# A two-block fp32 transformer on one core: two half groups at the end, a shorter first load, a conv tap moved to ACT and POOL, other planner durations

## What is computed

```python
def first_block(...):
    h = rms_norm(x, ln1)
    proj = h @ w_in                      # qkv_a, beta, decay, z, qkv_b, two gates
    y_a = gated_deltanet(qkv_a, ...) @ w_branch_a   # starts with the 4-tap conv below
    y_b = moba_attention(...) @ w_branch_b
    x = x + (sigmoid(gate_a) * y_a + sigmoid(gate_b) * y_b) @ w_out
    ...                                  # FFN with a 3-tap conv
def gated_deltanet(qkv, ...):
    qkv = silu(causal_dwconv(qkv, conv_w))          # 4 taps along the tokens, 3072 channels
    ...                                  # heads, chunks of 64 tokens
def second_block(...):
    z = rms_norm(x, attn_norm) @ w_in    # pool branch, RWKV7 with 16 heads
    x = x + concat(pool_out, rwkv_out) @ w_out
    x = x + square(relu(h2 @ w_ffn_up)) @ w_ffn_down
    gate = sigmoid(rms_norm(x, ple_norm) @ w_ple_gate)
    x = x + gate * (p @ w_ple_proj)
    return rms_norm(x, final_norm)
```

## Time and profile before

| | |
|---|---|
| median of 3 runs | 3005.75 us (3005.21 to 3009.81) |
| the profiled execution | 3008.47 us, its span 3006.7 us |
| mean granted clock of PE | 0.982 of full speed |
| busy: PE, DVE, ACT, POOL | 97%, 63%, 49%, 5% |
| read from HBM | 476.53 MB, 159 GB/s over the span |

### The profile page before, as it was taken

How to read it: one execution, slowest core, us unless ns; L and a number is a source line. 1 busy time by engine, 2 the same in 40 slices (tenths; PEclk the granted TensorE clock), 3 DMA queues, 4 the chain that set the end, 5 groups by cost and what they waited for, 6 DMA issues and landing times.

```text
span 3006.7 us, 55479 instructions
## 1 busy us (share of the span) xinstructions
PE 2919.0 (97%) x23504; PEld 2849.2 (95%) x23504; DVE 1908.6 (63%) x2146; ACT 1464.9 (49%) x1871; POOL 160.9 (5%) x136
## 2 busy tenths in 40 slices
PE   7998999999999999999999999998899999999998
PEld 7988989999999999999998999996899999999997
DVE  6467766555666667666777676664665555655665
ACT  5345555444554444444446555654544444444464
POOL 0010011000000000000001011111000000000000
PEclk9999999999999999999999999996999999999999
DMA  6644533665556665666565533330466666666654
GB/s 207 189 123 139 162 92 94 187 183 171 188 177 189 183 182 182 187 184 179 176 186 161 176 113 103 115 93 1 140 185 184 183 181 184 183 181 185 184 173 134
DMA packets 252104, 482.22 MB, mean 160 GB/s; under 512 B 16944, under 2 KB 22320, under 8 KB 251728
## 3 DMA queue, kind: packets, MB, share of 16 engines
q1 hardware_dynamic: 251856, 478.68, 53.2%
HBM read 476.53 MB, written 2.10 MB: 159 GB/s over the span
## 4 chain that ended last, share of the span: by engine, by line
PE 86%; DVE 7%; ACT 4%; DMA 2%; issue 1%; POOL 0%; DVEq 0%; SPq 0%; ACTq 0%; POOLq 0%
PE psm L411 78%; PE psb L470 7%; DVE slo L325 2%; DMA raw<-in_w_in 2%; ACT shi L315 1%; DVE ar L506 1%; DVE ar L498 1%; ACT ar L495 1%; PE psb L478 1%; DVE x L498 0%; ACT gf L495 0%; DMA raw<-in_w_out 0%; ACT L495 0%; DVE ar L509 0%; POOL ar L498 0%
## 5 line engine op out<-in xcount | busy, mean ns | idle before, releaser
L325 DVE TENSOR_TENSOR slo<-raw,shi 128x1024 fp32r<-128x1024 f32 (+1 forms) x901 | 1122.6, 1251 | 692.6 <-ACT shi L315 689.5
L315 ACT ACTIVATE shi<-raw 128x1024 fp32r<-128x1024 f32 (+1 forms) x901 | 946.6, 1054 | 1136.5 <-PE psm L411 897.2
L411 PE MATMUL psm<-gh,shi 128*128 128x256 f32 x3664 | 1050.7, 287 | 20.9 <-DVE slo L325 19.7
L411 PE MATMUL psm<-gl,shi 128*128 128x256 f32 x3664 | 1039.2, 284 | 0.0
L411 PE MATMUL psm<-gh,slo 128*128 128x256 f32 x3664 | 1039.1, 284 | 0.0
L411 PE MATMUL psm<-hh,shi 128*128 128x256 f32 x3408 | 974.5, 286 | 11.1 <-DVE slo L325 6.4
L411 PE MATMUL psm<-hh,slo 128*128 128x256 f32 x3408 | 966.4, 284 | 0.0
L411 PE MATMUL psm<-hl,shi 128*128 128x256 f32 x3408 | 966.4, 284 | 0.0
L411 PEld LDWEIGHTS psm<-gh,shi 128*128 128x128 f32 x3664 | 704.5, 192 | 28.7 <-DVE slo L325 22.6
L411 PEld LDWEIGHTS psm<-gl,shi 128*128 128x128 f32 x3664 | 704.6, 192 | 0.9 <-issue 0.3
L411 PEld LDWEIGHTS psm<-gh,slo 128*128 128x128 f32 x3664 | 704.1, 192 | 0.3
(11 more groups left out here) (190 smaller groups left out, 1304.9 us busy)
## 6 DMA issues: line engine op xcount, KB each, us to landing
raw<-in_w_in SPq DMA_DIRECT2D x240, 512.0 KB, 3.7
raw<-in_w_up SPq DMA_DIRECT2D x176, 512.0 KB, 4.0
raw<-in_w_ffn_up SPq DMA_DIRECT2D x128, 512.0 KB, 3.8
raw<-in_w_ffn_down SPq DMA_DIRECT2D x128, 512.0 KB, 4.2
raw<-in_w_down SPq DMA_DIRECT2D x88, 512.0 KB, 4.5
raw<-in_w_out SPq DMA_DIRECT2D x64, 512.0 KB, 4.2
raw<-in_w_ple_gate SPq DMA_DIRECT2D x32, 512.0 KB, 4.6
raw<-in_w_branch_b SPq DMA_DIRECT2D x16, 512.0 KB, 3.9
```

Of the source, the lines that this page charges most:

```text
L315: hi_tok[j] = A.do(lambda e: e.activation(shi[:, s, 0:m], raw[:, q, 0:m], ACT.Copy), landed, pe_tok.get(j - NS), chain=False, cost=0.22 + ...
L325: lo_tok[j] = V.do(lambda e: e.tensor_tensor(slo[:, s, 0:m], raw[:, q, 0:m], shi[:, s, 0:m].bitcast(F), ALU.subtract), landed, hi_tok[j], ...
L411: e.matmul(out, l, r, start=st, stop=sp, skip_group_check=True),
```

## The change

Four edits.

**Tail.** The last `pg` group of 512 columns becomes two of 256 columns. A tile then holds 4 blocks of rows by 256 columns: still 512 KB and still eight tiles, but rows of 1 KB instead of 2 KB in HBM. Each half has its own epilogue (`epi_half`). The sum of the earlier squares and of those of the first half is a background step (`sum_half`); the second half adds only its own. The last quarter of the output is scaled and stored in two pieces.

**Head.** The first load of `x` is split: blocks 0 and 1, weight tile 0, blocks 2 and 3, tile 1, then as before.

**Conv.** Tap 1 is no longer on DVE. Four more ACT scaled copies write it to `cth`, and one POOL tensor_tensor of 128 x 4 x 255 adds it to `dst`.

**Costs.** ACT's base goes from 0.22 to 0.25 us (0.33 with a scale from a tile), DVE's from 0.16 to 0.20, POOL's from 0.25 to 0.30, and scalar_tensor_tensor gets 0.05 more.

```diff
+            if g < 3:
+                gplan("pg", io["w_ple_gate_2"][0], 0, 512 * g, 512, 16)
+        for i in range(2):
+            gplan("pg", io["w_ple_gate_2"][0], 0, 1536 + 256 * i, 256, 16, kc=4)
...
-            return 0.25 + 2.0e-3 * columns(ap) if q is P else 0.16 + 1.04e-3 * columns(ap)
+            return 0.3 + 2.05e-3 * columns(ap) if q is P else 0.2 + 1.04e-3 * columns(ap)
...
         for f in range(4):
-            t_x.append(load(x[:, 4 * f:4 * f + 4, :], io["xt"][:, 4 * f:4 * f + 4, :]))
+            if f == 0:
+                t_x0 = load(x[:, 0:2, :], io["xt"][:, 0:2, :])
+                issue(0)
+                t_x.append(load(x[:, 2:4, :], io["xt"][:, 2:4, :]))
+                continue
             if f < NR:
                 issue(f)
+            t_x.append(load(x[:, 4 * f:4 * f + 4, :], io["xt"][:, 4 * f:4 * f + 4, :]))
...
                 for s in range(4):
-                    if s:
+                    o = dst if s == 0 else cth
+                    if s > 1:
...
                     for f in range(4):
-                        tq = act(dst[:, f, :], craw[:, f, :], ACT.Copy, tv, tt_["conv"],
-                                 scale=W("conv", 3 * 24 + 4 * g + f, 1))
+                        ta = act(o[:, f, s:256], craw[:, f, 0:256 - s], ACT.Copy, tv, tt_["conv"], g_tok.get(g - 1), tq,
+                                 scale=W("conv", (3 - s) * 24 + 4 * g + f, 1))
+                    if s:
+                        tq = tt(dst[:, :, s:256], dst[:, :, s:256], cth[:, :, s:256], ALU.add, ta, q=P)
                     yield
...
+        def sum_half():
+            while nf.n < 3 or 2 not in xw_tok:
+                yield
+            yield (x_tok[3], nf.tp[0])
+            sq = nf.sq[:, 0:512]
+            tq = act(sq.rearrange("p (a b) -> p a b", a=2), x[:, 12:14, :], ACT.Square, x_tok[3], nf.tp[0])
+            weigh((12, 13), 3, x_tok[3])
+            yield (tq,)
             b = bank()
...
+            mms([(b.ap[:, 0:256], C("ones"), s[:, 256 * k:256 * k + 256], k == 0 and s is nf.acc[0], False)
+                 for s, n in ((nf.acc[0], 4), (sq, 2)) for k in range(n)], nf.tp[0], tq, *b.free)
```

More of the change, by code:

```diff
@@ L213, in build @@
         s_raw = [sem(f"s_raw{i}") for i in range(NR)]
-        s_in = [sem(f"s_in{i}") for i in range(19)]
+        s_in = [sem(f"s_in{i}") for i in range(20)]
         s_out = sem("s_out")
@@ L483, in build, with acost @@
         table = [None]
-        def acost(ap, fn=ACT.Copy):
+        def acost(ap, fn=ACT.Copy, scale=1.0):
             own = {ACT.Sqrt: 1, ACT.Sin: 2, ACT.Ln: 3, ACT.Exp: 0, ACT.Tanh: 0}.get(fn, table[0])
@@ L488, in acost @@
             table[0] = own
-            return load + 0.22 + 0.82e-3 * columns(ap)
+            return load + (0.25 if isinstance(scale, float) else 0.33) + 0.82e-3 * columns(ap)
         def vcost(ap, q=None):
-            return 0.25 + 2.0e-3 * columns(ap) if q is P else 0.16 + 1.04e-3 * columns(ap)
+            return 0.3 + 2.05e-3 * columns(ap) if q is P else 0.2 + 1.04e-3 * columns(ap)
         def act(out, in_, fn, *tokens, scale=1.0, **kw):
-            return A.do(lambda e: e.activation(out, in_, fn, scale=scale, **kw), *tokens, cost=acost(out, fn))
+            return A.do(lambda e: e.activation(out, in_, fn, scale=scale, **kw), *tokens, cost=acost(out, fn, scale))
         def tt(out, a, b, op, *tokens, q=None):
@@ L505, in stt @@
         def stt(out, a, s, b, o1, o2, *tokens):
-            return V.do(lambda e: e.scalar_tensor_tensor(out, a, s, b, o1, o2), *tokens, cost=vcost(out))
+            return V.do(lambda e: e.scalar_tensor_tensor(out, a, s, b, o1, o2), *tokens, cost=0.05 + vcost(out))
         def rec(o, *tokens):
@@ L766, in build @@
         for j in range(NS):
-            nm.split((2 * j, 2 * j + 1), t_x[j // 2])
+            nm.split((2 * j, 2 * j + 1), t_x[j // 2] if j else t_x0)
             split_hi(j)
@@ L1059, in conv @@
                     for f in range(4):
-                        tq = act(dst[:, f, :], craw[:, f, :], ACT.Copy, tv, tt_["conv"],
-                                 scale=W("conv", 3 * 24 + 4 * g + f, 1))
+                        ta = act(o[:, f, s:256], craw[:, f, 0:256 - s], ACT.Copy, tv, tt_["conv"], g_tok.get(g - 1), tq,
+                                 scale=W("conv", (3 - s) * 24 + 4 * g + f, 1))
+                    if s:
+                        tq = tt(dst[:, :, s:256], dst[:, :, s:256], cth[:, :, s:256], ALU.add, ta, q=P)
                     yield
-                ta = act(cth, dst, ACT.Tanh, tq, g_tok.get(g - 1))
+                ta = act(cth, dst, ACT.Tanh, tq)
                 yield
+                V.wait(tq)
                 g_tok[g] = stt(dst, cth, 1.0, dst, ALU.add, ALU.mult, ta)
@@ L1860, in build, with weigh @@
         xw_tok = {}
-        def weigh(f):
-            for k in range(4 * f, 4 * f + 4):
-                xw_tok[f] = act(x[:, k, :], x[:, k, :], ACT.Copy, x_tok[f], scale=W("fn2", k, 1))
+        def weigh(ks, f, tok):
+            for k in ks:
+                xw_tok[f] = act(x[:, k, :], x[:, k, :], ACT.Copy, tok, scale=W("fn2", k, 1))
         def sum_up(f):
             yield from nf.squares(f, x_tok[f])
-            weigh(f)
+            weigh(range(4 * f, 4 * f + 4), f, x_tok[f])
             yield ()
@@ L1883, in epi_pg @@
             return epi
-        def epi_last(ps, tp):
-            bg_until(lambda: nf.n == 3 and 2 in xw_tok)
-            b = bank()
[L1889 to L1906, removed]
-                          for k in range(2)], tq)
[L1908 to L1911, removed]
@@ new lines, in build @@
+        last_sum = []
+        def sum_half():
[6 more added lines that the diff above has]
+            yield (tq,)
+            b = bank()
+            mms([(b.ap[:, 0:256], C("ones"), s[:, 256 * k:256 * k + 256], k == 0 and s is nf.acc[0], False)
+                 for s, n in ((nf.acc[0], 4), (sq, 2)) for k in range(n)], nf.tp[0], tq, *b.free)
+            last_sum.append(b)
+            yield ()
@@ new lines, in epi_half, with epi @@
+        def epi_half(i):
+            def epi(ps, tp):
+                bg_until(lambda: last_sum or not i)
+                th, xx = thb[:, 2 * i:2 * i + 2, :], x[:, 12 + 2 * i:14 + 2 * i, :]
+                tv = tt(th, ps[:, 0:512].rearrange("p (a b) -> p a b", a=2), bc(rb, 2), ALU.mult, tp)
+                ta = act(th, th, ACT.Tanh, tv, scale=0.5)
+                if i:
+                    act(pp1, C("eps", 0, 1), ACT.Sqrt)
+                stt(th, th, 1.0, ppb[:, 2 * i:2 * i + 2, :], ALU.add, ALU.mult, ta, pp_tok[-1])
+                x_tok[3 + i] = stt(xx, th, 0.5, xx, ALU.mult, ALU.add)
+                if not i:
+                    bgs[2].append(sum_half())
+                    return (tv,)
+                b, sq = last_sum[0], nf.sq[:, 512:1024]
+                tq = act(sq.rearrange("p (a b) -> p a b", a=2), xx, ACT.Square, x_tok[4])
+                tm = mms([(b.ap[:, 0:256], C("ones"), sq[:, 256 * k:256 * k + 256], False, k == 1)
+                          for k in range(2)], tq)
+                tr = act(rb, b.ap[:, 0:256], ACT.Sqrt, tm, scale=1.0 / D, bias=C("eps", 0, 1))
+                weigh((14, 15), 4, x_tok[4])
+                rec(rb, tr)
+                return (tv,)
+            return epi
@@ L1913, in build @@
         for g in range(4):
             group("pp", act_g(8), epi_pp, needs=(t_pp,))
-            group("pg", act_h, epi_pg(g) if g < 3 else epi_last)
+            if g < 3:
+                group("pg", act_h, epi_pg(g))
+        for i in range(2):
+            group("pg", act_h, epi_half(i))
+        parts = [(4 * f, 4 * f + 4, xw_tok[f]) for f in range(3)] + [(12, 14, xw_tok[3]), (14, 16, xw_tok[4])]
         tf = []
-        for f in range(4):
-            xx = x[:, 4 * f:4 * f + 4, :]
-            tf.append(tt(xx, xx, bc(rb, 4), ALU.mult, xw_tok[f]))
+        for a, e, t in parts:
+            tf.append(tt(x[:, a:e, :], x[:, a:e, :], bc(rb, e - a), ALU.mult, t))
@@ L1920, in build @@
         out_v = io["out"].rearrange("(c p) t -> p c t", p=128)
-        for c in range(4):
-            SP.dma(lambda e, c=c: e.dma_start(out_v[:, 4 * c:4 * c + 4, :], x[:, 4 * c:4 * c + 4, :]), s_out, tf[c])
+        for (a, e, _), t in zip(parts, tf):
+            SP.dma(lambda q, a=a, e=e: q.dma_start(out_v[:, a:e, :], x[:, a:e, :]), s_out, t)
             nout[0] += 1
```

1 line of the change is left out of this document (removed).

## The result

The changed kernel takes 3017.72 us (median of 5 runs, 3016.33 to 3021.73) beside 3005.75 us before (median of 5, 3002.57 to 3015.05); the ratio is 1.0031, interval 1.0018 to 1.0044. The two medians lie 12.0 us apart, more than the ratio says, so I go by ratio and interval. So it is 8 to 9 us slower. I had forecast 3008.4, no change, in a range from 2999 to 3016: the first median lies 1.7 us above its top, the second inside it, and the likeliest case (3005 to 3013) did not come true. Single runs of the kernel before spread from 2998 to 3018 us, so a stage's share has to be read from several traces.

The account below looks back on a forecast made before the run. PE, busy 97%, bounds the kernel: only its work, pauses and lowered clock count. Head 0, conv 0, reordered background 0, drain +2.4 and tail +0.2 give +2.6 on the median 3005.75: 3008.4 us, range 2999 to 3016.

Parts of the forecast that it names:

- the likeliest case: Whole kernel: the predicted sum of terms holds, 3005 to 3013 us; chance 0.50.
- Reordered background: 0: Background steps placed later by the new costs: small matmuls' sum unchanged, so 0 us, from −6 to +2.
- The conv: 0: Conv stretch, 204 to 345 us: moving tap 1 to ACT and POOL costs 0 us, from −3 to +12.
- the conv stretch gets shorter or longer by over 4 us: Sign that the prediction is wrong, for the stretch from 204 to 345 us.
- POOL's add locks DVE: Rival, conv: about four of six adds delay low splits by 2.1 us each; +8 to +12 us, 3015 to 3020; chance 0.15.
- The drain: 2023.7 to 2113 us: the output step stands 24 `psm` matmuls later and its chain keeps its length; +2.4 us, −3 to +6.
- The tail: Kernel end: six `psb` ahead of the last `psm` add 2.8 us, shorter work behind saves 2.5; +0.2, −0.8 to +1.5.
- The head: Kernel start: PE begins up to 1.0 us earlier but waits as much longer for the norm sum; 0, −1.0 to +0.3.

Follow-up runs that it names:

- The two removal runs: Costs and conv edits together on the kernel before, once with one ACT copy for tap 1's four (1.0015), once with tap 1's add on DVE, not POOL (1.0024).

## Why the prediction was right or wrong

**The step that failed: "Reordered background: 0".** I took the costs' reordering as a sum of small matmuls that stays the same, and priced only the waits (14.3 us missing in two stretches, of which some could be won). Means over the table's kernels give, for the new costs: from tile 54 to 132 333.2 us with the old conv for 336.8 with the old costs, −3.6; from 504 to 603 +3.7 (425.2 for 421.5). The second loss is not in a wait. As far as the traces tell it is the clock (13.7 us more at half), for which my step had no term: PE's pauses stay nearly as they were, but the matmuls came in lumps. My upper end of +2 was too low. The sum of the small matmuls is indeed the same, but not in each stretch: with the new costs the trace has 942 records of them from tile 504 to 603 where it had 972 or 976, and 382 in the drain for 354 (two records for each small matmul), while ten weight matmuls more stand ahead of tile 603. So the +3.7 came in spite of somewhat less work, and only the sum over the second block, below, can be compared.

**The second failure: that conv and costs add up.** "The conv: 0" holds with the old costs: 337.5 against 336.8 us. With the new costs the tap costs 7.3 us (340.5 against 333.2), and so takes back the costs' gain twice over. In whole runs the same interaction shows as 1.0025 for both edits beside 1.0002 and 0.9994 for each. By my own sign ("the conv stretch gets shorter or longer by over 4 us") I was wrong here too: tiles 54 to 132 took 4.1 and 6.6 us longer in the two traces of the changed kernel than in that of before. My working took one group's order and looked at the high split between the two sets of copies; there the split came first. In other groups a norm step stood in the same gap. The two removal runs gave back 5.0 us (fewer copies, and one locked low split less) and 3.2 us (no lock) in one trace each. They are not independent, since each shortens the same wait of PE, and in whole runs only the first may have given something back (1.0015, and 1.0024 for the second, beside 1.0025). So the tap behind the new order is shown as the cause in this stretch, and its division between copies and lock is not.

**The rival "POOL's add locks DVE"** had the right sign and size, 8 to 12 us, and its first condition came true (five low splits of six, where it wanted four). That it came near the measured time is luck: it was not the cause as stated, since each hit costs 1.3 us, not 2.1, with the old costs five such hits cost nothing, and part of the measured loss lies in the second block, where the conv is not. By the Trainium skill's rule (SBUF — State Buffer, Who interferes with whom) the second to be issued is fully blocked: the trace agrees, as the low split that started 0.98 us into POOL's add ended 1.08 us behind it, nearly its whole usual length. But what the block costs depends on whether PE waits behind it.

**The drain** was right in what moves and in part wrong in the rest. The chain goes through the output step in the changed kernel too, now right behind the last weight matmul:

```profile
2033.35 2.26 PE psb L473 x22
...
2035.99 1.28 ACT L498
```

In all six traces with the old costs this step starts 6.1 us ahead of the end of the last weight matmul, with 24 of them behind it; in the eight others it starts with that end. Predicted was +2.4 from the 24 weight matmuls; the means are 90.2 us for 86.7, +3.5, or +2.5 with the end of the stretch ahead of it (−1.0). That 2.5 is so near to 2.4 is partly luck, since the chain did not keep its length as I took it to: from the step to the next weight matmul it takes 90.2 us instead of 92.8. With the old costs that length goes from 89.6 to 95.4 us, and the half clock in it from 39 to 57 us. Behind the drain about 1.5 us came back: up to tile 880 it took 806.9 us and not 808.4. The clock does not explain this, it is at half for 5.1 us there for 5.0; PE is idle for 1.8 us instead of 3.1.

**The tail**: the term for six matmuls was 2.8 and measured 2.7 (67.9 for 65.2). Behind the last matmul I predicted 5.5 and the mean is 5.5, but the 8.0 us of before that I set against it was one execution with the clock at half. The mean of nine kernels with the old end is 6.9. So the gain was 1.5, not 2.5, and the tail is +1.2 instead of +0.2, in agreement with 1.0004. Taking a price at half clock from a single trace was the error.

**The head** was right in the mechanism: what PE gains at the start it waits longer. PE starts at 8.29 (predicted near 8.5) and waits 5.29 us for the norm sum instead of 4.59, and that wait ends 0.3 us later than before. Its price of 0 is not shown, since the head alone measured 3.6 us slower (interval 0.0 to 7.2):

```profile
8.29 0.58 PE L414 MATMUL psm<-gh,shi 128*128 128x256 f32 x1 [8.29 <-DVE slo L328]
...
39.97 1.62 PE L473 MATMUL psb<-ar,con 128*128 128x256 f32 x3 [5.29 <-DVE ar L501]
```

**The account.** First block +3.7 (340.5 for 336.8), RWKV stretch +3.7, its end −1.0 (from tile 603 to the drain 3.9 us for 4.9), drain +3.5, behind it −1.5, tail +1.2: +9.6 us. Left out are the head and the 372 tiles between the first two stretches, which took 1077.8 us with the new costs in the first block and 1077.1 with the old. Measured 8.1 to 9.3 by the two ratios. The same account gives −3.6 for the new costs in the first block (measured −5.4, interval −9.0 to −2.1), and +4.7 for them in the second (measured +7.8, interval +5.1 to +10.2), so up to 3 us of the last is not accounted for. Why these costs lump the steps in the second block and not in the first was not tried; it would need each cost changed by itself.

## What to carry to other kernels

Where a planner's numbers set the order, two edits that each do nothing can lose together, because they fill the same gap ahead of the same instruction: look at what stands between two high splits, not at each edit's price. Truer durations (a scaled copy takes 0.53 us; the old cost was 0.43, the new one 0.54) do not make a better order by themselves; they helped where PE waited and hurt where they gathered small matmuls into lumps, and keeping them for the first block alone gave 5.4 us. With PE at 97%, look for the stretches without large matmuls as well as for waits, because in these traces the clock fell in them. And where one trace of a kernel differs from the next by 2 or 3 us in a stretch, a gain of that size there is to be asked of the whole time as well.

## What the runs showed of the hardware

PE's clock fell although PE was busy 11.7 of 13.2 us, when the work was small matmuls, most of them on 64 of the 128 rows; the half clock came 6.7 us after the last large matmul and lasted 10.2 us (4.9 to 6.7 us after it in the eight traces with this stretch). Executions of the kernel before differ by up to 17 us in one set of runs. The drain alone took 83.5 to 89.3 us with the old costs: 89.1 and 89.3 where the clock was at half for 57 us of it, 83.5 to 87.4 where it was for 39 to 48. Whether that is the cause was not tried.
